# Token-major output projections with resident rows of the output matrix, in a two-block kernel on one Trainium2 core

## The reference, cut to what matters

```
block 1:  s = sig(g_a)*y_a + sig(g_f)*y_f + sig(g_c)*y_c        (the merge)
          x1 = rmsnorm(x + gt_l * (s @ w_out), final_g)
block 2:  u  = rms_norm(x1, norm_mix_pre); branches; merged = sum of gated branches
          h  = x1 + rms_norm(merged @ w_out_2, norm_mix_post)
          u  = rms_norm(h, norm_ffn_pre)
          out = h + rms_norm((silu(u @ Wg) * (u @ Wu)) @ w_down, norm_ffn_post)
```

## Time and profile before

| what | value |
|---|---|
| median of 3 runs | 3085.1 us (3081.94 to 3087.03) |
| profiled execution | 3083.83 us, span 3082.1 us |
| mean granted PE clock | 0.979 of full |

### The profile page before, as it was taken

How to read it: one execution, slowest core, us unless ns; L and a number is a source line. 1 busy time by engine, 2 the same in 40 slices (tenths; PEclk the granted TensorE clock), 3 DMA queues, 4 the chain that set the end, 5 groups by cost and what they waited for, 6 DMA issues and landing times.

```text
span 3082.1 us, 40975 instructions
## 1 busy us (share of the span) xinstructions
PE 2934.9 (95%) x15675; PEld 2365.4 (77%) x15675; DVE 1352.4 (44%) x2203; ACT 956.7 (31%) x1574; POOL 1016.1 (33%) x801
## 2 busy tenths in 40 slices
PE   5999989999999999999989999989878999999998
PEld 3788778888888877788677888758666888888886
DVE  5244430111011035544379999850663324324325
ACT  4344532222233244332453222352332111111113
POOL 3534312233333345222122333304554223223223
PEclk8999999999999999999999999999988999999999
DMA  5211021111112122111011111102220111111111
GB/s 206 51 39 39 18 79 54 48 48 41 54 50 92 51 92 86 51 36 53 24 37 37 46 46 51 39 37 70 76 62 28 48 48 48 48 48 48 48 48 75
DMA packets 261468, 169.42 MB, mean 55 GB/s; under 512 B 23604, under 2 KB 250605, under 8 KB 260205
## 3 DMA queue, kind: packets, MB, share of 16 engines
q1 hardware_dynamic: 259997, 162.65, 17.5%
q10 hardware_dynamic: 1360, 5.24, 0.4%
HBM read 159.41 MB, written 8.45 MB: 54 GB/s over the span
## 4 chain that ended last, share of the span: by engine, by line
PE 87%; DVE 6%; issue 2%; ACT 2%; POOL 1%; DMA 1%; SPq 0%; POOLq 0%; DVEq 0%; ACTq 0%
PE ps L326 69%; PE ps L3658 3%; PE ps L3657 3%; PE ps L3659 2%; PE ps L983 1%; PE ps L997 1%; DVE score L3076 1%; DVE ssq L1944 1%; DVE h_lo L1934 1%; PE ps L2480 1%; PE ps L3402 1%; PE ps L3392 1%; DMA rows<-in_norm_ffn_post 0%; PE ps L969 0%; PE ps L1523 0%
## 5 line engine op out<-in xcount | busy, mean ns | idle before, releaser
L326 PE MATMUL ps<-h_hi,w_hi 128*128 128x512 f32 x2864 | 1139.1, 398 | 35.3 <-DVE h_lo L1934 10.1
L326 PE MATMUL ps<-h_lo,w_hi 128*128 128x512 f32 x2864 | 1123.3, 392 | 0.0
L326 PE MATMUL ps<-h_hi,w_lo 128*128 128x512 f32 x2864 | 1122.3, 392 | 0.0
L310 POOL TENSOR_TENSOR w_lo<-raw,w_hi 128x512 fp32r<-128x512 f32 (+2 forms) x556 | 658.2, 1205 | 1296.9 <-ACT w_hi L303 1296.7
L326 PEld LDWEIGHTS ps<-h_hi,w_hi 128*128 128x128 f32 x2864 | 542.2, 189 | 157.9 <-issue 19.6
L326 PEld LDWEIGHTS ps<-h_hi,w_lo 128*128 128x128 f32 x2864 | 542.0, 189 | 116.4
L326 PEld LDWEIGHTS ps<-h_lo,w_hi 128*128 128x128 f32 x2864 | 542.6, 189 | 111.0 <-issue 1.0
L303 ACT ACTIVATE w_hi<-raw 128x512 fp32r<-128x512 f32 (+2 forms) x556 | 288.3, 567 | 865.2 <-PE ps L326 701.5
L3607 DVE TENSOR_TENSOR act<-gate,ps 128x1024 f32<-128x1024 f32 x22 | 26.9, 1221 | 446.1 <-PE ps L326 446.1
L3616 DVE TENSOR_TENSOR acc<-acc,ps 128x1024 f32<-128x1024 f32 x160 | 195.4, 1221 | 28.6 <-PE ps L3659 28.6
L1197 DVE TENSOR_TENSOR part<-sig,ps 128x1024 f32<-128x1024 f32 x40 | 48.6, 1215 | 339.1 <-PE ps L326 285.5
(11 more groups left out here) (434 smaller groups left out, 3406.5 us busy)
## 6 DMA issues: line engine op xcount, KB each, us to landing
raw<-in_w_in SPq DMA_DIRECT2D x88, 512.0 KB, 4.0
raw<-in_w_ffn_gate_up SPq DMA_DIRECT2D x44, 512.0 KB, 3.8
raw<-in_w_out SPq DMA_DIRECT2D x32, 512.0 KB, 3.7
raw<-in_w_gate SPq DMA_DIRECT2D x32, 512.0 KB, 4.1
raw<-in_w_ffn_down SPq DMA_DIRECT2D x22, 512.0 KB, 3.5
w_ada<-in_w_ada SPq DMA_DIRECT2D x8, 1024.0 KB, 10.7
x_tok<-in_x ACTq DMA_DIRECT2D x4, 1024.0 KB, 14.0
residual_gate<-in_w_ada SPq DMA_DIRECT2D x8, 512.0 KB
```

The source lines that it names most:

```text
L310: pool.tensor_tensor(w_lo[:, s, cut], raw[:, s, cut], w_hi[:, s, cut].bitcast(F32), ALU.subtract).then_inc(split.sem, 1)
L326: last = pe.matmul(dst, w[:, chunk[0] % 2, k], x(k), start=(k == ks[0] and n == 0), stop=(k == ks[-1] and n == 2))
```

## The change

Both projections hold activations and move rows of `w_out`. A chunk is now a row tile of the matrix, 128 input features x 1024 outputs. All eight rows stay on chip (`rows_hi`, `rows_lo`; rows 0 and 1 in the usual slots), so each is loaded, rounded and subtracted once. ACT rounds them, POOL makes their rests (`Rows.rest`; the parameter is called `dve`, the caller is POOL's block); DVE makes the rests of the sum (`sum_low`). PE does tokens 0 to 383 (three tiles) row by row while rows and rests arrive, and then the other five tiles one after the other, in `ps[0]` to `ps[2]`.

The result is token-major, so sums over features run along the free axis: ACT squares with a running sum, and the inverse root is a scalar for each partition. The gains become rows spread over partitions (`gate_row`, `final_row`, `pre_row`, `post_row`), loaded by DMA or, for the gate, made by two wide matmuls. The normalised tile goes back to feature-major by eight PE transposes (`turn`), through `ps[3]` alone; ACT rounds it out of `ps[3]` (`out_high`) and DVE subtracts (`out_low`). x, and in the second block the kept result, come in four 1 MB loads into the parts of `acc` whose sums have been used. The 64 transposes of x in the first projection and the 64 of the residual at the end of the feed-forward part are gone, and each projection gets 64 of its own result. PE's order after the last tile: turn 6, two quarters ahead, a third, turn 7, the fourth.

```diff
-                        dve.tensor_tensor(gate_t[:], ps[1][:, 0:KT], column("b_ada", 2 * KT, KT), ALU.add).then_inc(stat_ready.sem, 1)
+                        dve.tensor_tensor(gate_row[:], ps[1][:], gate_row[:], ALU.add).then_inc(stat_ready.sem, 1)
...
+                        for c in (0, HALF):
+                            last = pe.matmul(ps[1][:, c:c + HALF], ones[:], residual_gate[:, 0, c:c + HALF], start=True, stop=True)
...
+        ROW_ORDER = (6, 7, 4, 5, 2, 3, 0, 1)
+        FEW = 3
...
+        class Rows:
+
+
...
+            def weights(self, m):
+                return [wide_row(x[:, m]) for x in (w_hi, w_lo)] if m < 2 else [self.high[:, m - 2], self.low[:, m - 2]]
+
+            def load(self, sp, m, source):
+                sp.wait_ge(rounded.sem, half_after(rounded, m - 2, 1, 0, 0))
+                sp.wait_ge(split.sem, half_after(split, m - 4 if m >= 4 else m - 2 - m % 2, 1, 0, 0))
+                dst, src = source(self.raw(m))
+                sp.dma_start(dst, src).then_inc(loaded[m % 2].sem, 16)
+
+            def round(self, act, m):
+                act.wait_ge(loaded[m % 2].sem, loaded[m % 2].at((chunks[0] + m - m % 2) // 2 + 1))
+                for c in (0, HALF):
+                    act.activation(self.weights(m)[0][:, c:c + HALF], wide_row(self.raw(m))[:, c:c + HALF], ACT.Copy)\
+                       .then_inc(rounded.sem, 1)
+
+            def rest(self, dve, m):
+                for half, c in enumerate((0, HALF)):
+                    dve.wait_ge(rounded.sem, half_after(rounded, m, half, 0, 0))
+                    hi, lo = self.weights(m)
+                    dve.tensor_tensor(lo[:, c:c + HALF], wide_row(self.raw(m))[:, c:c + HALF], hi[:, c:c + HALF].bitcast(F32),
+                                      ALU.subtract).then_inc(split.sem, 1)
+
+        def first_tokens(x, n):
...
+
+        def other_tokens(x, n):
+            return x[:, ROW_ORDER[n], FEW * P:]
+
+        def tile_of(x, t):
+            return x[:, :, t * P:t * P + P]
+
+        def by_feature(bank):
+            return bank[:].rearrange("p (k c) -> p k c", c=P)
...
+                if n == 5:
+                    act.wait_ge(used.sem, after(used, -1, 0, 0))
+                    rows.round(act, 1)
+                    rows.round(act, 2)
+            rows.round(act, 3)
+            rows.round(act, 4)
+            for m in range(5, KT):
+                rows.round(act, m)
+                for n in range(2 * (m - 5), 2 * (m - 5) + 2):
+                    high(other_tokens, n, y_hi)
+            for n in range(6, KT):
+                high(other_tokens, n, y_hi)
...
+            for n in range(KT):
+                low(first_tokens, n, hi_ready, lo_ready)
+            for n in range(KT):
+                low(other_tokens, n, y_hi, lo_ready2)
...
+
+            pe.wait_ge(*gates[1])
+            for m in range(6):
+                pe.wait_ge(hi_ready.sem, hi_ready.at(m + 1))
+                for t in range(FEW):
+                    for half, c in enumerate((0, HALF)):
+                        if t == 0:
+                            rows_ready(m, half)
+                        step(t, m, c, 0)
+                        step(t, m, c, 1)
+                pe.wait_ge(lo_ready.sem, lo_ready.at(m + 1))
+                for t in range(FEW):
+                    for c in (0, HALF):
+                        step(t, m, c, 2)
+            pe.wait_ge(lo_ready.sem, lo_ready.at(KT))
+            for t in range(FEW):
+                for m in (6, 7):
+                    for half, c in enumerate((0, HALF)):
+                        if t == 0:
+                            rows_ready(m, half)
+                        for n in range(3):
+                            done = step(t, m, c, n, m == 7)
+                done.then_inc(o_ready.sem, 1)
+            pe.wait_ge(lo_ready2.sem, lo_ready2.at(KT))
+            for t in range(FEW, TT):
+                pe.wait_ge(evicted.sem, evicted.at(t - 2))
+                for m in range(KT):
+                    if m == 4 and t < 5:
+                        turn(2 * t - 6)
+                    for c in (0, HALF):
+                        for n in range(3):
+                            done = step(t, m, c, n, m == KT - 1)
+                    if t == TT - 1 and m == 0:
+                        done.then_inc(used.sem, KT - 1)
+                    if t == TT - 1 and m == 1:
+                        done.then_inc(used.sem, 1)
+                done.then_inc(o_ready.sem, 1)
+                turn(2 * t - 5 if t < 5 else t - 1)
+            pe.wait_ge(evicted.sem, evicted.at(TT - 1))
+            ahead(pe, KT, 0, 0)
+            ahead(pe, KT, 0, 1)
+            pe.wait_ge(evicted.sem, evicted.at(TT))
+            ahead(pe, KT, 1, 0)
+            turn(TT - 1)
+            ahead(pe, KT, 1, 1)
...
+                    for m in range(2, KT):
+                        rows.load(sp, m, project_source(w)(0, m))
...
+                    for n in range(4):
+                        sp.wait_ge(lo_ready2.sem, lo_ready2.at(2 * n + 2))
+                        at = ROW_ORDER[2 * n]
+                        sp.dma_start(acc[:, at:at + 2], x_rows[:, 2 * n:2 * n + 2]).then_inc(xt_loaded[n].sem, 16)
+                    for t in range(TT):
+                        if t == 5:
+                            for m in range(2):
+                                load_chunk(sp, KT + m, 0, 0, following(0, m))
+                        sp.wait_ge(mod_ready.sem, mod_ready.at(t + 1))
+                        sp.dma_start(kept[:, t], x_of(t)).then_inc(stored.sem, 16)
...
+                    for m in range(1, KT):
+                        rows.rest(pool, m)
...
+                    for t in range(TT - 1):
+                        inverse(t)
+                    rest_chunk(pool, KT, 0, 0)
+                    rest_chunk(pool, KT + 1, 0, 0)
+                    inverse(TT - 1)
...
+                    def squares(t):
+                        act.wait_ge(y_ready.sem, y_ready.at(t + 1))
+                        act.wait_ge(sq_ready.sem, sq_ready.at(2 * t))
+                        act.activation(junk, tmp[:, t % FEW], ACT.Square, accum_out=sums[:, t, 0:1]).then_inc(sq_ready.sem, 1)
+                        act.wait_ge(y_ready2.sem, y_ready2.at(t + 1))
+                        act.wait_ge(sq_ready.sem, sq_ready.at(2 * t + 1))
+                        act.activation(junk, x_of(t), ACT.Square, accum_out=sums[:, t, 1:2]).then_inc(sq_ready.sem, 1)
...
+                    def keep(t):
+                        act.wait_ge(h_ready.sem, h_ready.at(t + 1))
+                        act.activation(x_of(t), x_of(t), ACT.Copy, scale=rstd[:, t, 0:1]).then_inc(mod_ready.sem, 1)
...
+                    def out_high(t):
+                        act.wait_ge(transposed.sem, transposed.at(t + 1))
+                        act.activation(tile_of(h_hi, t), by_feature(ps[3]), ACT.Copy).then_inc(y_ready3.sem, 1)
...
+                    out_high(0)
+                    squares(3)
+                    out_high(1)
+                    keep(3)
+                    out_high(2)
+                    for t in range(4, TT):
+                        squares(t)
+                        out_high(t - 1)
+                        if t == TT - 2:
+                            round_chunk(act, KT, 0, 0)
+                            round_chunk(act, KT + 1, 0, 0)
+                        keep(t)
+                    out_high(TT - 1)
...
+                    def add(t):
+                        x, y = tmp[:, t % FEW], x_of(t)
+                        dve.wait_ge(o_ready.sem, o_ready.at(t + 1))
+                        if t >= FEW:
+                            dve.wait_ge(transposed.sem, transposed.at(t - FEW + 1))
+                        dve.tensor_tensor(x, ps[t % 3][:], gate_row[:], ALU.mult).then_inc(evicted.sem, 1)
+                        dve.wait_ge(xt_loaded[t // 2].sem, xt_loaded[t // 2].at(1))
+                        dve.wait_ge(evicted.sem, evicted.at(t + 1))
+                        dve.tensor_tensor(x, x, y, ALU.add).then_inc(y_ready.sem, 1)
+                        dve.wait_ge(y_ready.sem, y_ready.at(t + 1))
+                        dve.tensor_tensor(y, x, final_row[:], ALU.mult).then_inc(y_ready2.sem, 1)
...
+                        dve.scalar_tensor_tensor(out=var[:, t], in0=s, scalar=1.0 / D, in1=eps[:],
+                                                 op0=ALU.mult, op1=ALU.add).then_inc(stat_ready.sem, 1)
...
+                    def normed(t):
+                        dve.wait_ge(norm_ready.sem, norm_ready.at(t + 1))
+                        dve.scalar_tensor_tensor(out=tmp[:, t % FEW], in0=x_of(t), scalar=rstd[:, t, 1:2], in1=pre_row[:],
+                                                 op0=ALU.mult, op1=ALU.mult).then_inc(h_ready.sem, 1)
...
+                    def out_low(t):
+                        dve.wait_ge(y_ready3.sem, y_ready3.at(t + 1))
+                        dve.tensor_tensor(tile_of(h_lo, t), by_feature(ps[3]), tile_of(h_hi, t).bitcast(F32), ALU.subtract)\
```

(59 more changed lines are left out.)

782 lines of the change are left out of this document (237 added, 545 removed).

## The result

The changed kernel takes 3010.65 us (median of 4 runs, 3010.16 to 3012.9), the kernel before 3083.52 beside it (3080.61 to 3087.03): ratio 0.9765, 95% interval 0.9748 to 0.9782. Forecast: 3020, range 3005 to 3042. The profiled execution of the changed kernel is the one of 3010.16; against the 3083.83 of before that is 73.7 less, where the sum gave 65.0.

A forecast was written before the change was run, and what follows sets the result against it. The prediction took PE (TensorE) as the bound. Its terms, -9.4 and -50.7 for the projections, -1.6 and -2.6 for the entries, -0.7 for the feed-forward end, took 3083.8 to 3018.8; plus 1.3 for the median, 3020 us, range 3005 to 3042.

The forecast's parts named there:

- the sum gave 65.0: Whole kernel: the forecast's savings in both projections, next-stage entries and feed-forward end, together -65.0 us.
- PE's queue: Each projection: 384 row-form products at 0.2334 us, turns 7.0, work ahead 10.9; floor 107.5 us.
- The 0.216 that led to 3006: Matmul spacing by the Trainium skill's rule for 512 columns; 13.5 us less for 768 products, rejected for the measured spacing.
- Start: Each projection's start, from T (end of the preceding merge's last product): waits 4.5 us, tile 0 done at T+32.4.
- Middle: Later tiles, where turns wait for ps[3] to be emptied: PE waits 4.5 us in first projection, 1.0 in second.
- The clock cost of 1.9: First projection: slower granted clock after the 4.5 us wait at turn 1 costs another 1.9 us, charged once.
- End: From last tile's end to next stage: 13.2 us in first projection with a 0.5 wait, 12.7 in second without.
- Entries: Next stages after both projections: PE enters without having stood, clock 1.00, saving 1.6 and 2.6 us.
- End of the feed-forward part: 64 residual transposes go, but DVE sets the pace there, so only early gaps go: -0.7 us.
- the rival with shorter waits: Whole kernel: products at 0.2279 us, start waits 2.5, no clock loss, giving 3010 us; chance 0.13.

The follow-up runs named there:

- bank_by_bank: Changed kernel with tiles 3 to 7 of both projections doing all 24 matmuls of the first 512 columns, then the other 24; 3011.92 us.
- end_turns_back: Changed kernel with the 64 residual transposes put back on PE at the end of the feed-forward part, their result unread; 3010.9 us.
- rests_swapped: Changed kernel with start work exchanged: POOL makes the rests of the sum, DVE those of the matrix rows; 3016.89 us.

## Why the prediction was right, step by step

- **PE's queue.** 384 products at 0.2334: measured 11.16/48 = 0.2325, 0.3 less in all. Turns 0.87 as forecast. The 0.216 that led to 3006 is shorter than any stream of this type in the runs. (The section of the Trainium skill's TensorE: Matmul & The Clock Gate that the prediction names, Back-to-back issue gap, gives it for a matmul by itself, and 0.131 for a stream of weight loads and matmuls; the traces agree with neither.)
- **Start.** Tile 0 done at T+32.4: measured T+32.75 and T+31.1. The sum was right by luck, its parts were not: waits 2.9 and 2.4, not 4.5, because row 7 was there at T+28.4, not 31.7. (The waits that the prediction lists, 2.4, 1.3 and 1.2, add up to 4.9; its 4.5 is the difference of T+32.4 and T+27.9.) POOL's half rests took 1.59 (row 1) to 1.88, where I had 1.8 to 2.1. In the first projection the clock, which I had kept at 1.00, made up the difference: 0.76 in the profiled execution, so that 100 products took 25.20, where 23.62 were possible (bank_by_bank). In bank_by_bank and end_turns_back it stayed up, and the projection is 118.2.
- **Middle.** The wait of 4.5 at turn 1 was 4.42, and its releaser DVE `h_lo`; in the second projection 1.1 for 1.0. The cause I named, two `keep` ahead of `out_high(0)`, is only half of it: without them 2.8 remain. The clock cost of 1.9 was 1.07 on the turn and some 1.1 on the next 24, 2.2. The changed kernel's clock after the wait for row 1 and around turn 1 (columns as in the earlier trace rows):

```profile
1106.00:1112.00 6.00, 4.04 (x11) 0.76 0.44 152
...
1154.00:1160.00 6.00, 4.09 (x14) 0.50 0.22 87
```

- **End.** 13.2 and 12.7: measured 14.1 and 12.7. DVE's sum for the last tile took 1.91 in place of 1.23, beside POOL's rests for the next stage, so the wait was 1.3 and not 0.5. The sum had these rests in POOL's queue, but no price for them on DVE. DVE's queue there:

```profile
1207.24 1.23 DVE L1797 TENSOR_TENSOR tmp<-ps,gate_row 128x1024 f32<-128x1024 f32 x1 [1.48 <-PE ps L1640]
1208.57 1.91 DVE L1800 TENSOR_TENSOR tmp<-tmp,acc 128x1024 f32<-128x1024 f32 x1
```

- **Entries.** -1.6 and -2.6: the clock is 1.00 in both, where the kernel before had 0.75 in the six us from its first entry (1232 to 1238) and, by the earlier trace rows, 0.50 at its second:

```profile
1219.00:1225.00 6.00, 6.00 (x28) 1.00 0.97 276
...
2270.00:2276.00 6.00, 6.00 (x28) 1.00 0.01 3
```

84 matmuls take 19.11 and 156 take 35.39, 0.2275 and 0.2269 each.
- **End of the feed-forward part.** -0.7 came (43.2 us from the last `act` on, 43.9 before), but not from the transposes, which cost 0.1; more likely from the residual's copies, which went with them and which no run tried alone.
- **What the sum lacks.** The stages between were priced at 1.6, their entry, and gave 7.9; about 3 us of it lie at the load in memory attention, the rest is open. So the measured 3010.65 lies at the lower edge of the 3010 to 3032 that the prediction called its own, for a reason that the prediction hasn't got. The number was that of the rival with shorter waits, but not for its reasons: the spacing stayed, and the clock did cost.

## What to carry to other kernels

Where a stage on PE ends in a chain of small steps, count what PE could do in that time and put it there: the four quarters were worth 18 us in two stages. Where a serial statistic over features stands at the end of a stage, try to move the sums from partitions to the free axis: the second projection went from 65.3 us above its products and the quarters to 11.6 (111.8 - 384 x 0.2325 - 10.9). No run tried that layout without the other parts of the change, such as the rows kept on chip, so their shares aren't shown. And a gain of under 5 us in one stage can be lost in the total: read it from the length of that stage.

## What the runs showed of the hardware

- A short wait of PE may or may not lower the clock behind it. The wait of 2.9 us for row 1 gave 25.2 us for 100 matmuls in six executions, 26.3 in one and 23.6 in two, without a change in the waits.
- DVE and POOL side by side, each subtracting two SBUF tiles of 512 columns, take 1.87 (DVE in rests_swapped) and 1.59 to 1.88 us (POOL in the changed kernel), where alone they take 0.69 and 1.28. Exchanging their work changes the length of the projections by 1 us at most.
- The stages between differ by up to 7.7 us (939.0 to 946.7) among twelve executions that have the same code there.
